# The halves of the row sums added on VectorE in a two-layer decoder trunk: four products per norm in place of eight

## The chip, the cores and the metric

The kernel runs on one core of one Trainium2 chip. The metric is device time in microseconds (us) of one launch; where several runs are given, their median. Engines are named as in the profile: PE (TensorE matmul), PEld (its weight loads), DVE (VectorE), ACT (ScalarE), POOL (GpSimd) and SP (SyncE).

## The reference

The input is one sequence of 512 tokens with 1024 channels, fp32. Cut to what matters here:

```
def rms_norm(x, g):
    xf = x.astype(jnp.float32)
    y = xf * lax.rsqrt(jnp.mean(xf * xf, axis=-1, keepdims=True) + EPS)
    return (y * g.astype(jnp.float32)).astype(x.dtype)

Each layer (DEPTH = 2):
  h = RMSNorm(x)
  p = h @ W_in      (mixer A: chunked spatial gating; mixer B: latent attention with
                     a rotary key; mixer C: gated DeltaNet with a short causal conv;
                     three merge gates)
  y_i = branch_i(p) @ W_branch[i]
  x = x + (sum_i sigmoid(gate_i) * y_i) @ W_out
  x = x + W2 relu(W1 RMSNorm(x))^2
```

Two norms per layer take the mean of the squares of each token's 1024 channels: four norms in all, called norm 0 (input of layer 0), norm 1 (feed-forward of layer 0), norm 2 (input of layer 1) and norm 3 (feed-forward of layer 1). The change concerns how these sums of squares are completed.

## The kernel before, in words

**Layout and products.** Tokens lie on the free axis: a projection gives a PSUM tile of 128 channels x 512 tokens. Each fp32 factor is split in a high part and the rest (`hHi`/`hLo` for the activations, `wHi`/`wLo` for the weights), and each product is three matmuls (L662 to L664). A projection tile takes 8 steps of three, 24 matmuls of 128x512. Tiles of the combined input projection come in a fixed order: tile 0 ("misc": decay, beta and rotary key rows), tiles 1 to 4 (`k`), 5 to 8 (`q`), 9 to 12 (`v`), and so on. From tile 5 on they use two PSUM banks in turn: `project` (L709 on) waits on `bank_read[n % 2]` until the last tile in that bank has been read, so tile 7 starts after the third reading of an odd tile, which are tiles 1, 3 and 5.

**Weights.** They stream from memory in units of 512 KB into `wraw` (two slots). POOL makes of each unit the high part `wHi` (L562, a tensor_scalar) and the rest `wLo` (L567, a tensor_tensor of `wraw` and `wHi`) in a ring of four slots, as fast as units land and slots come free.

**The norm.** PE transposes the stream 128x128 at a time (L681), ACT makes `hHi` (L1344), DVE `hLo` (`stream_low`, L1801), and the projections begin before the norm's factor is known: it is multiplied in when DVE reads a projection tile. ACT squares the rows of the untransposed stream in two halves of 512 channels (L1332), and its accumulator leaves one sum per token and half in `rowsq[P, 2, TT]` (128 partitions, 2 halves, 4 token tiles). `sum_stream` (L684) then waits for all eight squares of the norm and, for each of the four token tiles, multiplies the column `rowsq[:, half, t]`, broadcast to 128x128, by the identity, for both halves into the same PSUM columns: the two halves are added in PSUM, and every partition receives the row of the 128 tokens' sums. From that ACT makes `rstdT` (L1360 a logarithm, L1362 an exponential), and signals `rstd_ready`.

```
for t in range(TT):
    for half in range(2):
        last = mm(S(2)[:, t * P:(t + 1) * P], rowsq[:, half, t:t + 1].broadcast_to([P, P]), ident, start=half == 0, stop=half == 1)
```

**DVE's program at the start.** The order of the work is written out by hand, one program per engine, and each engine executes its program in order, waiting on semaphores. DVE makes `hLo` (L1801 x8), then a triangular table `tri` (L1844), `lowrow` (L1845, L1847), and `rotation_angles(0)` (L1820 to L1837: a cast and seven small operations of 128x64, each waiting for the one before). Then it waits for `rstd_ready` and reads tile 0 (`xrow` L1898, `krT` L1900, L1902). `conv(i)` then takes the tiles k0 to k3, q0 to q3 and v0 in turn: it scales the PSUM tile by `rstdT` (L1909), multiplies it by the last tap (L1913), adds three shifted products (L1916 x3) and counts `bank_read`. Behind `conv(0)` stands L1944, behind `conv(2)` L1947, L1948 and L1950 (the decay rows), behind `conv(5)` a few copies and `rotation_angles(1)`. So tile 7's `bank_read` count of three is reached when `conv(4)` ends.

**Other norms.** In norms 1 and 3 DVE adds the residual (`add_stream`, L1808) half by half and makes four `hLo` tiles after each half; in norm 2 it makes all eight after the last feed-forward group.

**Memory.** The tiles of SBUF are placed in order; `FRONT` and `BACK` are paddings that keep the tiles behind them at fixed places.

Of the kernel before, what the change touches and what calls it, by code (L numbers as in the profile page):

```python
# [10 lines left out]
ALU = mybir.AluOpType  # L11
# [4 lines left out]
P = 128  # L16
# [3 lines left out]
TT = SEQ // P  # L20
# [112 lines left out]
LOW, STACK = 32, 32 + HEADS  # L133


FRONT, BACK = 1664, 348


PRM = {}
# [25 lines left out]
class PerLayer:  # L165
# [3 lines left out]

    y_stored = 16; prm_loaded = 16; x_loaded = 16  # L170

    h_lo = 16; h_high = 16; rows_squared = 16; stat_summed = 2; rl_done = 2; rstd_ready = 2

    act_tile = 12; csq_ready = 8; csq_summed = 2; ksum_copied = 2; ksum_turned = 2

# [37 lines left out]
def hybrid_trunk(nc, stream, params, x, positions, constants, out):  # L213

    with ExitStack() as ctx:
        def sb(name, shape, dt=F32):
            return ctx.enter_context(nc.sbuf_tensor(name, shape, dt))

        def sem(name):
            return ctx.enter_context(nc.semaphore(name))  # L220
# [18 lines left out]
        headstat = sb("headstat", [P, 3, TT * HEADS])  # L239
        negmax, unused = sb("negmax", [P, 2]), sb("unused", [P, 2])  # L240
        psums, pinv = sb("psums", [P, 2, HEADS]), sb("pinv", [P, 2, HEADS])
        rowsq = sb("rowsq", [P, 2, TT])


        sb("back", [P, BACK // 4])
# [59 lines left out]
        def c(name, i=0, n=None, parts=P):  # L305
            a, b = CST[name]
            return cst[0:parts, a + i * (n or 0):(a + (i + 1) * n if n else b)]

        def p(name, i=None, parts=P):
            a, b = PRM[name]  # L310
            return prm[0:parts, a:b] if i is None else prm[0:parts, a + i:a + i + 1]

        ident = c("ident")
# [13 lines left out]
        y_stored, prm_loaded, x_loaded = sem("y_stored"), sem("prm_loaded"), sem("x_loaded")  # L327

        h_lo, h_high, rows_squared = sem("h_lo"), sem("h_high"), sem("rows_squared")
        stat_summed, rl_done, rstd_ready = sem("stat_summed"), sem("rl_done"), sem("rstd_ready")  # L330

        act_tile, csq_ready, csq_summed = sem("act_tile"), sem("csq_ready"), sem("csq_summed")
# [93 lines left out]
        def sums_bank(d):  # L426

            return ps[:, 2 + d % 6]

        def stream_bank(norm, d):  # L430

            return ps[:, (4, 5, 4, 5, 6, 7, 2, 3)[d]] if norm % 2 else sums_bank(d)

        def halves(half):

            return np.s_[half * 512:(half + 1) * 512]
# [214 lines left out]
        def _(pe):  # L651
            pe.wait_ge(ident_in, 16)
            for layer in range(DEPTH):
                mm = nc.tensor.matmul

                def S(n):
                    return ps[:, 2 + n]

                def passes(o, l, lc, r, rc, start, stop):

                    (lh, ll), (rh, rl) = l, r
                    mm(o, lh[lc], rh[rc], start=start, stop=False)  # L662
                    mm(o, lh[lc], rl[rc], start=False, stop=False)  # L663
                    return mm(o, ll[lc], rh[rc], start=False, stop=stop)  # L664
# [18 lines left out]

                def sum_stream(norm):  # L684

                    pe.wait_ge(rows_squared, 8 * norm + 8)
                    pe.wait_ge(h_lo, 8 * norm + 3)
                    for t in range(TT):
                        for half in range(2):
                            last = mm(S(2)[:, t * P:(t + 1) * P], rowsq[:, half, t:t + 1].broadcast_to([P, P]), ident, start=half == 0, stop=half == 1)  # L690
                    last.then_inc(stat_summed, 1)

                def wide_sums(half, kk):
# [293 lines left out]
                if layer == 0:  # L987
                    turn_stream(0, range(0, 4))
                    high_step(0, 0)
                    high_step(0, 1)  # L990
                    turn_stream(0, range(4, 6))
                    high_step(1, 0)
                    high_step(1, 1)
                    high_step(0, 2)
                    turn_stream(0, range(6, KD))
                    high_step(1, 2)
                    for k in range(3, KD):
                        high_step(0, k)
                        high_step(1, k)
                        if k >= 4:  # L1000
                            low_step(0, 2 * k - 8)
                            low_step(0, 2 * k - 7)
                    sum_stream(0)
                    for k in range(KD):
                        low_step(1, k)
                else:
                    project(("misc", 0))
                    sum_stream(2 * layer)
# [35 lines left out]
                for t in range(TT):  # L1044
                    last = nc.tensor.transpose(S(4)[:, t * ROPE:(t + 1) * ROPE], krT[:, t * P:(t + 1) * P], c("ident", parts=ROPE)[:, 0:ROPE])
# [6 lines left out]
                for t in range(TT):  # L1052
                    last = mm(S(3)[32 * t:32 * t + 32, 0:P], c("ones")[:, 0:32], klsq[:, 1, t * P:(t + 1) * P], start=True, stop=True)
# [3 lines left out]
                for t in range(TT + 1):  # L1057
                    last = nc.tensor.transpose(S(5)[:, t * P:(t + 1) * P] if t < TT else S(4)[:, P:2 * P], lsums[:, t * P:(t + 1) * P], ident)
# [12 lines left out]
                for n in range(2):  # L1071
# [3 lines left out]
                    for t in range(TT):  # L1075
# [3 lines left out]
                        for k in range(2):  # L1079
                            last = passes(S(g % 4), (latHi, latLo), np.s_[:, 3 + k, t * P:(t + 1) * P],  # L1080
                                          (wHi, wLo), np.s_[:, slot, k * 512:(k + 1) * 512], k == 0, k == 1)
# [184 lines left out]
                ff1(0, range(0, 4))  # L1266
                turn_stream(2 * layer + 1, range(4, KD))
                sum_stream(2 * layer + 1)
                ff1(1, range(0, 4))
                ff1(0, range(4, KD))  # L1270
# [505 lines left out]
        def _(dve):  # L1776
# [10 lines left out]
            def sums_ready(d, full, done):  # L1787

                if d % 4 < 3:
                    dve.wait_ge(sums_full, full + d // 4 * 3 + d % 4 + 1)  # L1790
                else:
                    dve.wait_ge(unit_done, done + d // 4 * 4 + 4)

            def stream_low(norm, columns=range(KD)):

                gain = "g2" if norm % 2 else "g1"
                if norm % 2 == 0:
                    dve.wait_ge(prm_loaded, 16 * (norm // 2 + 1))
                for d in columns:
                    dve.wait_ge(h_high, 8 * norm + d + 1)  # L1800
                    nc.vector.scalar_tensor_tensor(hLo[:, d], stream_bank(norm, d), p(gain, d), hHi[:, d].bitcast(F32), ALU.mult, ALU.subtract).then_inc(h_lo, 1)  # L1801

            def add_stream(half, full, done):

                for t in range(TT):
                    sums_ready(4 * half + t, full, done)
                    part = y[:, t, halves(half)]
                    nc.vector.tensor_tensor(part, part, sums_bank(4 * half + t), ALU.add).then_inc(x_added, 1)  # L1808

            def zero_rows():  # L1810

                nc.vector.memset(rowsr[0:64].bitcast(F32), 0.0)
                nc.vector.memset(gone[:], 0.0).then_inc(vector_step, 1)
                dve.wait_ge(vector_step, steps.next())

            def rotation_angles(n):
# [22 lines left out]
                assert n == 0 or turns.n == ROPE_STEPS, turns.n  # L1839

            zero_rows()
            stream_low(0)
            dve.wait_ge(tables_in, 48)
            nc.vector.tensor_scalar(tri[:], c("incl"), -1.0, None, ALU.is_ge).then_inc(tri_done, 1)  # L1844
            nc.vector.reduce_sum(lowrow[:], c("ident")[0:2 * HEADS, HEADS:2 * HEADS], AX.X).then_inc(vector_step, 1)  # L1845
# [4 lines left out]
            for layer in range(DEPTH):  # L1850
# [439 lines left out]
                dve.wait_ge(x_loaded, layer * per.x_loaded + 16)  # L2290
                for half in range(2):
                    add_stream(half, layer * per.sums_full, layer * per.unit_done + UNIT_NO[("out", 0)])
                    stream_low(2 * layer + 1, range(4 * half, 4 * half + 4))

                def rectify(n):
# [88 lines left out]
                if layer < DEPTH - 1:  # L2384
                    zero_rows()
# [6 lines left out]
                add_corner(g, "p3", Y, 0, 1, ALU.subtract, (g, "p6"))  # L2392
                if layer < DEPTH - 1:
                    stream_low(2 * layer + 2)


# [122 lines left out]
```

## Time and profile before

| | |
|---|---|
| runs | 1763.55, 1764.39, 1763.82 us; median 1763.82 |
| profiled execution, its own time | 1764.11 us |
| its span | 1762.3 us |
| granted TensorE clock | 1.00 |
| PE busy | 1744.1 us, 99% of the span |
| POOL / DVE / ACT busy | 1066.3 / 958.8 / 689.9 us |

The profile is of one execution. Its page gives each engine's busy time, the span in 40 slices, and the chain of work that ended last. The answers of the trace are lists of single instructions (the timeline), of waits, and of groups. In the timeline an instruction that is held up once it has started shows as longer than its like; an engine that waits on a semaphore shows as idle, in brackets with what released it.

### The profile page before, as it was taken

To read this page: it belongs to the slowest core of one execution; us is meant where nothing else is said; L and a number is where in the kernel's file an instruction comes from. 1 tells how busy PE (TensorE), PEld (TensorE's weight loads), DVE (VectorE), ACT (ScalarE), POOL (GpSimd) and SP (SyncE) were. 2 spreads that over 40 slices of the span, in tenths; PEclk is the share of its full clock that TensorE was granted. 3 is DMA by queue.
4 is the path that set the end of the run, shared out by engine and by line. 5 is a ranking of instruction groups with operands and counts; after the bars stand their busy time and mean duration, and the time that the engine had idled before them with its cause. 6 is when DMAs were issued, how large, how long until landed. Compare 5 with 4: busy or idle time off the path is not lost.

```text
span 1762.3 us, 26300 instructions
## 1 busy us (share of the span) xinstructions
PE 1744.1 (99%) x10006; PEld 1426.3 (81%) x10006; DVE 958.8 (54%) x1565; ACT 689.9 (39%) x1241; POOL 1066.3 (61%) x572
## 2 busy tenths in 40 slices
PE   8999999999999999999999999999999999999999
PEld 7778888778888888888787788887788888888887
DVE  6786636653542455444576866266443435444445
ACT  6433316650104444444355243075411054444442
POOL 6444367235665777777774434662456657777776
PEclk9999999999999999999999999999999999999999
DMA  6222133123235666666542222331332356666655
GB/s 201 85 69 77 49 96 108 37 96 96 84 97 169 157 172 161 161 174 157 130 156 78 71 70 61 96 96 37 108 96 85 97 158 163 159 173 158 169 154 144
DMA packets 58897, 207.18 MB, mean 118 GB/s; under 512 B 6369, under 2 KB 8705, under 8 KB 58785
## 3 DMA queue, kind: packets, MB, share of 16 engines
q1 hardware_dynamic: 47520, 164.94, 29.9%
q0 software_dynamic: 9216, 33.56, 10.2%
q10 hardware_dynamic: 2048, 7.10, 1.1%
q8 instruction: 80, 1.31, 0.3%
q14 instruction: 33, 0.26, 0.0%
HBM read 184.61 MB, written 4.19 MB: 107 GB/s over the span
## 4 chain that ended last, share of the span: by engine, by line
PE 95%; ACT 2%; DVE 2%; issue 1%; DMA 0%; SPq 0%; DVEq 0%; ACTq 0%
PE ps L662 22%; PE ps L664 22%; PE ps L663 22%; PE ps L1259 6%; PE ps L1261 6%; PE ps L1260 6%; PE ps L1131 2%; PE ps L1140 1%; PE ps L1153 1%; PE ps L681 1%; PE ps L904 1%; PE ps L891 0%; DMA xin<-x 0%; PE ps L941 0%; PE ps L1203 0%
## 5 line engine op out<-in xcount | busy, mean ns | idle before, releaser
L662 PE MATMUL ps<-hHi,wHi 128*128 128x512 f32 x1360 | 553.2, 407 | 1.3 <-DVE convd L1916 1.3
L664 PE MATMUL ps<-hHi,wLo 128*128 128x512 f32 x1360 | 530.4, 390 | 0.0
L663 PE MATMUL ps<-hLo,wHi 128*128 128x512 f32 x1360 | 529.8, 390 | 0.0
L562 POOL TENSOR_SCALAR wHi<-wraw 128x1024 fp32r<-128x1024 f32 x168 | 181.4, 1080 | 497.3 <-PE ps L664 480.2
L567 POOL TENSOR_TENSOR wLo<-wraw,wHi 128x1024 fp32r<-128x1024 f32 x168 | 415.2, 2472 | 13.9
L593 POOL TENSOR_TENSOR wLo<-w,wHi 128x1024 fp32r<-128x1024 f32 x96 | 239.2, 2514 | 138.6 <-ACT wHi L1690 138.0
L662 PEld LDWEIGHTS ps<-hHi,wHi 128*128 128x128 f32 x1360 | 255.4, 188 | 61.5 <-issue 6.9
L663 PEld LDWEIGHTS ps<-hLo,wHi 128*128 128x128 f32 x1360 | 255.7, 188 | 54.7 <-issue 3.8
L664 PEld LDWEIGHTS ps<-hHi,wLo 128*128 128x128 f32 x1360 | 255.3, 188 | 54.2
L1259 PE MATMUL ps<-wHi,fHi 128*128 128x512 f32 x448 | 174.8, 390 | 1.8 <-issue 1.8
L1260 PE MATMUL ps<-wLo,fHi 128*128 128x512 f32 x448 | 174.3, 389 | 0.0
L1261 PE MATMUL ps<-wHi,fLo 128*128 128x512 f32 x448 | 174.3, 389 | 0.0
L593 POOL TENSOR_TENSOR wLo<-wraw,wHi 128x1024 fp32r<-128x1024 f32 x56 | 144.3, 2576 | 14.2 <-ACT wHi L1690 14.2
L2302 DVE SCALAR_TENSOR_TENSOR relu<-ps,rstdT 128x512 f32<-128x512 f32 x64 | 44.2, 691 | 187.0 <-PE ps L664 187.0
L1709 ACT ACTIVATE ps<-relu 128x512 f32<-128x512 f32 x64 | 38.5, 602 | 269.9 <-DVE relu L2302 269.9
L1396 ACT ACTIVATE sg<-ps 128x512 f32<-128x512 f32 x48 | 28.8, 599 | 255.7 <-DVE ps L1859 255.7
L2337 DVE TENSOR_TENSOR y<-y,ps 128x1024 f32<-128x1024 f32 x98 | 116.7, 1212 | 6.7 <-PE ps L1261 6.5
L1690 ACT CAST wHi<-w 128x1024 fp32r<-128x1024 f32 x96 | 99.5, 1043 | 22.4 <-DMA w<-w 18.9
L1259 PEld LDWEIGHTS ps<-wHi,fHi 128*128 128x128 f32 x448 | 84.1, 188 | 20.7 <-issue 2.8
L1859 DVE TENSOR_TENSOR ps<-ps,rstdT 128x512 f32<-128x512 f32 x56 | 38.9, 698 | 111.2 <-PE ps L664 111.0
L1261 PEld LDWEIGHTS ps<-wHi,fLo 128*128 128x128 f32 x448 | 84.1, 188 | 17.5
L1260 PEld LDWEIGHTS ps<-wLo,fHi 128*128 128x128 f32 x448 | 84.1, 188 | 17.3
(334 smaller groups left out, 2675.0 us busy)
## 6 DMA issues: line engine op xcount, KB each, us to landing
wraw<-stream SPq DMA_DIRECT2D x224, 512.0 KB, 3.6
w<-stream SPq DMA_DIRECT2D x64, 512.0 KB, 4.4
w<-w POOLq DMA_DIRECT2D x32, 512.0 KB, 6.9
b<-stream SPq DMA_DIRECT2D x16, 512.0 KB, 3.5
b<-stream POOLq DMA_DIRECT2D x16, 512.0 KB, 6.4
w<-stream POOLq DMA_DIRECT2D x16, 512.0 KB, 8.1
xin<-x SPq DMA_DIRECT2D x4, 512.0 KB, 6.8
y<-x ACTq DMA_DIRECT2D x1, 2048.0 KB, 9.9
```

Of the source, the lines that this page charges most:

```text
L562: nc.gpsimd.tensor_scalar(wHi[:, slot], wraw[:, slot % RAW], 1.0, 0.0, ALU.mult, ALU.add).then_inc(unit_high, 1)
L567: nc.gpsimd.tensor_tensor(wLo[:, slot], wraw[:, slot % RAW], wHi[:, slot].bitcast(F32), ALU.subtract).then_inc(unit_split, 1)
L593: nc.gpsimd.tensor_tensor(wLo[:, at % RING], source, wHi[:, at % RING].bitcast(F32), ALU.subtract).then_inc(unit_split, 1)
L662: mm(o, lh[lc], rh[rc], start=start, stop=False)
L663: mm(o, lh[lc], rl[rc], start=False, stop=False)
L664: return mm(o, ll[lc], rh[rc], start=False, stop=stop)
L1259: mm(ps[:, bank + i], fHi[b][tokens], wHi[cols], start=opens and k == 0, stop=False, skip_group_check=True)
L1260: mm(ps[:, bank + i], fHi[b][tokens], wLo[cols], start=False, stop=False, skip_group_check=True)
L1261: last = mm(ps[:, bank + i], fLo[b][tokens], wHi[cols], start=False, stop=k == 1, skip_group_check=True)
L1690: nc.scalar.copy(wHi[:, at % RING], source).then_inc(high_copied, 1)
L2302: stt(relu[:, n % 2], tile_home(n), 0.0, rstdT[:], ALU.max, ALU.mult).then_inc(vector_tile, 1)
L2337: tt_(part, part, ps[:, bank:bank + 2], op).then_inc(corner_added, 1)
```

## The change

A new tile `rowsum[P, TT]` (16 bytes per partition) holds the sum of both halves. DVE adds them (`sum_rows`), once per norm, and counts a new semaphore, `rows_summed`; PE's `sum_stream` waits for that in place of `rows_squared` and makes one product for each token tile. `BACK` is 16 bytes smaller, so the tiles behind it keep their addresses. For norm 0, `sum_rows` stands between the `hLo` tiles and `tri`; for norms 1 and 3 between the second half's residual additions and its `hLo` tiles; for norm 2 behind the `hLo` tiles.

```diff
-FRONT, BACK = 1664, 348
+FRONT, BACK = 1664, 332
...
-        rowsq = sb("rowsq", [P, 2, TT])
+        rowsq, rowsum = sb("rowsq", [P, 2, TT]), sb("rowsum", [P, TT])
...
                 def sum_stream(norm):
 
-                    pe.wait_ge(rows_squared, 8 * norm + 8)
+                    pe.wait_ge(rows_summed, norm + 1)
                     pe.wait_ge(h_lo, 8 * norm + 3)
                     for t in range(TT):
-                        for half in range(2):
-                            last = mm(S(2)[:, t * P:(t + 1) * P], rowsq[:, half, t:t + 1].broadcast_to([P, P]), ident, start=half == 0, stop=half == 1)
+                        last = mm(S(2)[:, t * P:(t + 1) * P], rowsum[:, t:t + 1].broadcast_to([P, P]), ident, start=True, stop=True)
                     last.then_inc(stat_summed, 1)
...
+            def sum_rows(norm):
+
+                dve.wait_ge(rows_squared, 8 * norm + 8)
+                if norm:
+                    dve.wait_ge(stat_summed, norm)
+                nc.vector.tensor_tensor(rowsum[:], rowsq[:, 0], rowsq[:, 1], ALU.add).then_inc(rows_summed, 1)
+
...
             zero_rows()
             stream_low(0)
+            sum_rows(0)
             dve.wait_ge(tables_in, 48)
             nc.vector.tensor_scalar(tri[:], c("incl"), -1.0, None, ALU.is_ge).then_inc(tri_done, 1)
...
                     add_stream(half, layer * per.sums_full, layer * per.unit_done + UNIT_NO[("out", 0)])
+                    if half:
+                        sum_rows(2 * layer + 1)
                     stream_low(2 * layer + 1, range(4 * half, 4 * half + 4))
...
                 if layer < DEPTH - 1:
                     stream_low(2 * layer + 2)
+                    sum_rows(2 * layer + 2)
```

The order of the instructions shows what that moves. First PE's, at norm 0, between the last steps of the first tiles; - is before, + the change, and `cst` is the table that holds the identity:

```order
 L731 MATMUL ps<-hLo,wHi 128x512
 L736 MATMUL ps<-hHi,wLo 128x512 x2
-L690 MATMUL ps<-cst,rowsq 128x128 x8
+L690 MATMUL ps<-cst,rowsum 128x128 x4
 L736 MATMUL ps<-hHi,wLo 128x512 x8
```

Four products are gone there, and in the same way at each of the other three norms.

Second DVE's at norm 0, before the change, with the semaphores that each instruction waits for:

```order
L1801 SCALAR_TENSOR_TENSOR hLo<-ps,prm,hHi 128x512 [waits h_high] x7
L1844 TENSOR_SCALAR tri<-cst 128x128 [waits tables_in]
L1845 TENSOR_REDUCE lowrow<-cst 16x1
L1847 TENSOR_SCALAR lowrow<-lowrow 16x1 [waits vector_step]
L1820 CAST posf<-posi 128x4 [waits tables_in,vector_step]
L1824 TENSOR_TENSOR gy<-posf,cst 128x64 [waits rope_step]
L1827 TENSOR_SCALAR gy<-gy 128x64 [waits rope_step]
L1829 TENSOR_SCALAR gy<-gy 128x64 [waits rope_step]
L1832 SCALAR_TENSOR_TENSOR gy<-gy 128x64 [waits rope_step] x3
L1837 TENSOR_SCALAR trig<-gy 128x64 [waits rope_step]
L1898 SCALAR_TENSOR_TENSOR xrow<-ps,sgn,rstdT 40x512 [waits rstd_ready,unit_done,rope_step]
```

And the same stretch with the change:

```order
L1801 SCALAR_TENSOR_TENSOR hLo<-ps,prm,hHi 128x512 [waits h_high] x7
L1815 TENSOR_TENSOR rowsum<-rowsq 128x4 [waits rows_squared]
L1852 TENSOR_SCALAR tri<-cst 128x128 [waits tables_in]
L1853 TENSOR_REDUCE lowrow<-cst 16x1
L1855 TENSOR_SCALAR lowrow<-lowrow 16x1 [waits vector_step]
L1827 CAST posf<-posi 128x4 [waits tables_in,vector_step]
L1831 TENSOR_TENSOR gy<-posf,cst 128x64 [waits rope_step]
L1834 TENSOR_SCALAR gy<-gy 128x64 [waits rope_step]
L1836 TENSOR_SCALAR gy<-gy 128x64 [waits rope_step]
L1839 SCALAR_TENSOR_TENSOR gy<-gy 128x64 [waits rope_step] x3
L1844 TENSOR_SCALAR trig<-gy 128x64 [waits rope_step]
L1906 SCALAR_TENSOR_TENSOR xrow<-ps,sgn,rstdT 40x512 [waits rstd_ready,unit_done,rope_step]
```

The eleven small instructions now stand behind the addition, and so behind its wait for ACT's eighth square.

Third DVE's at norm 1 with the change; norm 3 reads the same:

```order
L1808 TENSOR_TENSOR y<-y,ps 128x512 [waits sums_full] x3
L1808 TENSOR_TENSOR y<-y,ps 128x512 [waits unit_done]
L1815 TENSOR_TENSOR rowsum<-rowsq 128x4 [waits stat_summed,rows_squared]
L1801 SCALAR_TENSOR_TENSOR hLo<-ps,prm,hHi 128x512 [waits h_high] x4
L2312 SCALAR_TENSOR_TENSOR relu<-ps,rstdT 128x512 [waits rstd_ready,unit_done]
```

The addition is the one new row; four `hLo` tiles stand behind it. At norm 2 it follows the last `hLo` tile. The programs of ACT, POOL and SP are the same as before.

## Rows read from the trace of the kernel before

**Rows 1.** The page: busy times, granted clock in 40 slices, the chain by engine

```profile
PE 1744.1 (99%) x10006; PEld 1426.3 (81%) x10006; DVE 958.8 (54%) x1565; ACT 689.9 (39%) x1241; POOL 1066.3 (61%) x572
...
PEclk9999999999999999999999999999999999999999
...
PE 95%; ACT 2%; DVE 2%; issue 1%; DMA 0%; SPq 0%; DVEq 0%; ACTq 0%
```

**Rows 2.** Waits of PE: engine, line, cause: us in total, times, longest

```profile
PE ps L662 <- DVE convd L1916: 1.3, 2, 0.6
```

**Rows 3.** Instructions that read rowsq: count, duration ns min/median/max, first and last start

```profile
L690 PE MATMUL ps<-cst,rowsq x64: 271/275/275, 20.9 to 1433.5; 128*128 128x128 f32 x64
```

**Rows 4.** Chain that ended last, norm 0: start us, us, what

```profile
21.07 1.78 PE ps L690 x16
```

**Rows 5.** Timeline of PE at norm 0: start us, us, instruction

```profile
20.91 1.95 PE L690 MATMUL ps<-cst,rowsq 128*128 128x128 f32 x16
22.61 2.09 PE L736 MATMUL ps<-hHi,wLo 128*128 128x512 f32 x8
```

**Rows 6.** Timeline of ACT and DVE at norm 0: [idle before <-releaser] in brackets

```profile
18.66 0.20 ACT L1332 ACTIVATION_READ_ACCUMULATOR squares<-xin 128x1 f32 x1
...
16.51 0.22 DVE L1844 TENSOR_SCALAR tri<-cst 128x128 f32<-128x128 f32 x1
...
25.66 0.74 DVE L1898 SCALAR_TENSOR_TENSOR xrow<-ps,sgn,rstdT 40x512 f32<-40x512 f32 x1 [6.77 <-ACT rstdT L1362]
```

**Rows 7.** Timeline of POOL, 18 to 34 us

```profile
18.95 1.05 POOL L562 TENSOR_SCALAR wHi<-wraw 128x1024 fp32r<-128x1024 f32 x1 [3.58 <-DMA wraw<-stream]
20.09 2.36 POOL L567 TENSOR_TENSOR wLo<-wraw,wHi 128x1024 fp32r<-128x1024 f32 x1
...
23.54 2.40 POOL L567 TENSOR_TENSOR wLo<-wraw,wHi 128x1024 fp32r<-128x1024 f32 x1
26.24 1.06 POOL L562 TENSOR_SCALAR wHi<-wraw 128x1024 fp32r<-128x1024 f32 x1 [0.30 <-DMA wraw<-stream]
27.38 2.52 POOL L567 TENSOR_TENSOR wLo<-wraw,wHi 128x1024 fp32r<-128x1024 f32 x1
29.86 1.06 POOL L562 TENSOR_SCALAR wHi<-wraw 128x1024 fp32r<-128x1024 f32 x1
31.01 2.40 POOL L567 TENSOR_TENSOR wLo<-wraw,wHi 128x1024 fp32r<-128x1024 f32 x1
```

**Rows 8.** L1902 in both layers, and POOL beside the second (timeline)

```profile
L1902 DVE TENSOR_SCALAR xrow<-xrow,prm x2: 474/1570/2666, 27.2 to 898.5; 8x512 f32<-8x512 f32 x2
...
898.52 2.40 POOL L567 TENSOR_TENSOR wLo<-wraw,wHi 128x1024 fp32r<-128x1024 f32 x1
```

**Rows 9.** Timeline of DVE, 31 to 53 us

```profile
31.42 2.54 DVE L1944 SCALAR_TENSOR_TENSOR arow<-xrow 40x512 f32<-40x512 f32 x1
...
41.43 1.48 DVE L1948 SCALAR_TENSOR_TENSOR xrow<-xrow,arow 40x512 f32<-40x512 f32 x1
42.94 2.50 DVE L1950 TENSOR_SCALAR xrow<-xrow,slope 40x512 f32<-40x512 f32 x1
...
50.62 2.32 DVE L1916 SCALAR_TENSOR_TENSOR convd<-ps,prm,convd 128x511 f32<-128x511 f32 x3
```

**Rows 10.** Timeline of PE where tile 7 starts

```profile
53.20 0.50 PE L662 MATMUL ps<-hHi,wHi 128*128 128x512 f32 x1
```

**Rows 11.** Timeline of POOL and PE at norm 1

```profile
553.61 2.38 POOL L567 TENSOR_TENSOR wLo<-wraw,wHi 128x1024 fp32r<-128x1024 f32 x1
...
556.56 1.95 PE L690 MATMUL ps<-cst,rowsq 128*128 128x128 f32 x16
```

**Rows 12.** Timeline of POOL and PE at norm 2

```profile
890.89 1.05 POOL L562 TENSOR_SCALAR wHi<-wraw 128x1024 fp32r<-128x1024 f32 x1 [0.55 <-DMA wraw<-stream]
...
892.32 1.95 PE L690 MATMUL ps<-cst,rowsq 128*128 128x128 f32 x16
```

**Rows 13.** Timeline of PE at its first products

```profile
5.49 3.34 PE L681 MATMUL ps<-cst,xin 128*128 128x128 f32 x16 [5.49 <-DMA xin<-x]
```

More of the change, by code:

```diff
@@ L170 @@
     y_stored = 16; prm_loaded = 16; x_loaded = 16
-    h_lo = 16; h_high = 16; rows_squared = 16; stat_summed = 2; rl_done = 2; rstd_ready = 2
+    h_lo = 16; h_high = 16; rows_squared = 16; rows_summed = 2; stat_summed = 2; rl_done = 2; rstd_ready = 2
     act_tile = 12; csq_ready = 8; csq_summed = 2; ksum_copied = 2; ksum_turned = 2
@@ L329, in hybrid_trunk @@
         h_lo, h_high, rows_squared = sem("h_lo"), sem("h_high"), sem("rows_squared")
+        rows_summed = sem("rows_summed")
         stat_summed, rl_done, rstd_ready = sem("stat_summed"), sem("rl_done"), sem("rstd_ready")
```

## The prediction

> **What bounds the kernel now.** I read the page first. PE is busy for 99% of the span at a granted clock of nine tenths or more in all 40 slices, and the chain that ended last runs over PE for 95% [rows 1]. So time is won by fewer PE instructions, and lost where PE is made to wait. The list of PE's waits says how near that is: only the wait on `conv` (L1916) bears on this change, twice and 1.3 us in all, 0.6 us at the longest [rows 2]. DVE has gaps over the whole program (54% busy), but the question is the stretch around norm 0. There I read the timelines of ACT, DVE, POOL and PE side by side [rows 5 to 10].
>
> What bounds the end there is a chain: squares (ACT), sums (PE), `rstdT` (ACT), `xrow` (DVE), then nine `conv`s on DVE, whose fifth releases the bank that PE needs for tile 7. The last piece of `conv(4)` starts at 50.62 and its group of three takes 2.32, so it ends at 52.94; PE starts tile 7 at 53.20 [rows 9, 10]. **The slack is 0.26 us.** From `xrow` on DVE is almost never idle up to there, so what delays `xrow` reaches PE, less what is won back on the way.
>
> A second thing is to be seen there. Some DVE instructions last until a running POOL instruction ends. L1902 (8x512, SBUF to SBUF) takes 0.474 in layer 0 and 2.666 in layer 1, where it starts together with an L567 of 2.40 [rows 8]. L1944 takes 2.54 from 31.42, and the L567 beside it ends at 33.41 [rows 7, 9]. L1948 and L1950, one after the other, take 1.48 and 2.50 [rows 9]: each waits for one POOL instruction. So with both engines at work they take turns, one DVE instruction per POOL instruction. Instructions that read PSUM (L1909, L1913, L1916) show none of it. The Trainium skill, page "SBUF — State Buffer", section "Who interferes with whom", says that VectorE and GpSimd share a pair of SBUF ports as an exclusive lock held for a whole instruction, and that a VectorE operation with two SBUF inputs takes part; the 2.666 against 0.474 agrees.
>
> **The change part by part.**
>
> *Products removed.* There are 64 records of L690, 16 per norm for 8 products, so two records to a product [rows 3]. On the chain 16 cost 1.78 us, 0.111 each [rows 4]; by the timeline the next line starts 1.70 after the first, 0.106 each [rows 5]. Eight fewer records save 0.85 to 0.89 per norm. I take 0.89, and 3.56 for four norms, if each reaches the end.
>
> *Additions at norms 1, 2 and 3.* No row shows a 128x4 addition. The bounds are nothing (hidden) and, for one norm, the 2.40 of an L567 that it falls behind. At norm 1 an L567 runs from 553.61 to 555.99 [rows 11]. The addition ends behind it at about 556.1, and PE comes to the sum at 556.56, or not before: hidden, by 0.4. Norm 3 has the same pattern. The `hLo` tiles behind the addition wait for ACT anyway. At norm 2 the L562 ends at 891.94, and PE comes at 892.32 [rows 12]: hidden again, by 0.3 if the addition is let in between L562 and the next POOL instruction, which the turns above say. PE comes earlier nowhere by more than the norms before have saved, and POOL's work, which follows PE's freeing of slots, moves along. So these three give −0.89 each, **−2.67**. If norm 2's addition lands behind the next L567, of 2.4, the cost is some 1.6 us instead; that goes to a rival.
>
> *The addition at norm 0.* ACT's last square ends at 18.86, and POOL's L562 starts at 18.95 [rows 6, 7]. The addition fits before it, or waits until 20.00. PE comes to the sum at 20.91 [rows 5], so PE is not held up in either case, and `rstdT` comes 0.89 earlier.
>
> *The eleven small instructions moved behind it.* This is the costly part. Before, they start at 16.51 and end by 18.9 [rows 6], while POOL is idle: its L562 at 18.95 had stood 3.58 us idle [rows 7]. They cost nothing, as DVE then waits 6.77 us for `rstdT` [rows 6]. Now they stand behind the addition, and POOL works back to back from 18.95. Their bounds: 2.4 us as before if nothing holds them up, so they end at 21.4 and still cost nothing; or one POOL instruction each. By the turns: `tri` comes behind L562 (20.0), the two `lowrow` pieces of 16 channels by one element beside it, the cast behind L567 (22.45), the first product behind L562 (23.45), the first scaling behind L567 (25.94). In POOL's gap of 0.30 before 26.24 [rows 7] two more slip in. The remaining three come behind 27.30, 29.90 and 30.92. So DVE is free at about **31.0**. I take this end, since the rows on L1948 and L1950 are the nearest, though they are wider (512 elements against 64).
>
> `xrow` then starts at 31.0 in place of 25.66: 5.3 late. From there: `xrow` and `krT` 1.4, then L1902 behind the L567 that ends at 33.41 (before it had met none, 0.47): 33.5 to 33.7, and `conv(0)` is 6.0 late. L1944 was held up before by 1.8 us (2.54 less the 0.74 that the equally large L1898 takes [rows 6, 9]), and now, at 37.4, meets at most the end of an L562 of 1.06: 4.9 late. L1948 and L1950 were held up for 2.8 us in all, by 0.74 and 0.47 alone, and now, shifted against POOL, for some 2.3: 4.4 late. `conv(4)` ends at 57.3 in place of 52.94, and PE starts tile 7 at 57.4 in place of 53.20: **+4.2**. The 0.89 that PE wins at norm 0 is swallowed by this wait, so it is not in the sum.
>
> *Later in layer 0.* `rotation_angles(1)` behind `conv(5)` may now touch a POOL instruction; bounds 0 and 0.9, I take **+0.4**.
>
> *The new padding* leaves the addresses as they are: nothing.
>
> **Sum:** +4.2 + 0.4 − 2.67 = +1.9 us. The profiled execution took 1764.11 us (span 1762.3 and 1.8 around it), 0.29 above the median of the runs; the difference is added to the median 1763.82: **1765.7 us**. A measurement of this kernel can tell 0.2% (3.5 us) from no change, so the lines lie at 1760.3 and 1767.3, and my forecast is in between: no change that can be told, though 1.9 slower.
>
> **The rivals.**
>
> *A. The small instructions are not held up* (or only the addition is): the change does what it says, −3.56 us, **1760.3**. For it: they are short, and no row shows an instruction of 64 elements beside POOL in this stretch. Against: L1902, of 8 channels, was held up for 2.2 us. It is decided by whether DVE is free before 24.8, when `rstdT` now comes. Chance 0.13, of which 0.09 below 1760.3.
>
> *B. Some slip through.* If two or three pass between POOL's instructions, DVE is free at 26 to 27.5 and PE stands still for 0.5 to 1.5: **1761.8** to 1763. Chance 0.10.
>
> *C. A longer lag.* If nothing slips into the gap before 26.24, the last comes behind the L567 that ends at 33.41; `conv(0)` then ends after 40, and PE's tile 5, which takes the bank that it releases, waits as well; or norm 2's addition falls behind L567 (+1.6). Total +3.5 to +4.3: **1767.4 to 1768.1**. For it: two POOL instructions of 2.4 us are only 1.1 apart. Chance 0.12, all on the slower side.
>
> *D. The lag of the forecast, and TensorE's clock falls in it.* This ends slower. PE would stand still for some 4 us ahead of tile 7. Before, it stands so long only at the very start, 5.49 us [rows 13]. That start shows the price: the first 16 records of 128x128 take 3.34 us against 1.95 for 16 of the same shape later [rows 5], so 1.4 us; up to 2.8 if it stays low twice as long. Total +3.3 to +4.7: **1767.1 to 1768.5**. For it: the stop is long. Against: between the stops PE has short products to do (the sums of `csq`), and the granted clock never fell in the 40 slices [rows 1]. It decides from the point where the clock is below 1.0 in the stretch after the stop. The Trainium skill, page "TensorE: Matmul & The Clock Gate", section "What's actually happening", says that the throttled state is the default and that activity releases it, which speaks for D; the slow first products agree. Chance 0.15, slower.
>
> **How the numbers follow.** Forecast 0.50, B 0.10, C 0.12, D 0.15, A 0.13. Slower by over 0.2%: C and D, 0.27. Faster: 0.09. Same: 0.50 + 0.10 + the 0.04 left of A, 0.64. The range starts at 1761.6, just under B, and leaves out A (0.13). At the other end it takes in D's and C's bounds, with 0.5 for the unknown rotation: 1769.0. The forecast's own range is 1764.5 to 1767.0.
>
> **What would show it.** In the profile after: 32 records of L690, four times 0.89 long. DVE's small instructions stretch from 18.9 to about 31, several of them 1 to 2.5 us long and ending with a POOL instruction; `xrow` starts near 31 and waits for nothing; a wait of PE's L662 on L1924 (`conv`) of 4 to 5 us ahead of tile 7, partly before the `csq` sums. If `xrow` starts at 24.8 behind `rstdT`, I am wrong and A is right. If PE's stop is there but the time is over 1767, the clock and norm 2's sum are the places to look: a start later than 893 less the shift of the first half would be the second. From 60 us on everything should run as before, 4 to 5 us late, until norms 1 to 3 give 0.89 each back.

## The result, and the profile after

The changed kernel takes 1779.62 us (median of six runs, 1777.8 to 1785.19) against 1764.01 us for the kernel before (median of six, 1763.55 to 1765.66). The ratio is 1.0092, 95% interval 1.0082 to 1.0102: **slower by 0.9%**, where 1765.7 was forecast. The profiled execution took 1785.19 us (span 1783.3), the slowest of the six and 21.1 us above the profiled execution of before. The runs lie 7 us apart, those of before 2. The granted clock on record is 0.998 for the profiled run, 0.999 for one other (1780.38) and 1.000 for the remaining four, so the profile shows the second loss below at its largest, not as the median has it.

The page of the changed kernel, busy times and granted clock, answers to [rows 1]:

```profile
PE 1760.4 (99%) x9974; PEld 1424.6 (80%) x9974; DVE 971.2 (54%) x1569; ACT 690.0 (39%) x1241; POOL 1067.8 (60%) x572
...
PEclk9999999999999999999999999999999999999999
```

PE has 32 instructions fewer, and is busy for 16.3 us more. Waiting is the smaller part of the loss. The list of PE's waits (us in total, times, longest), which answers to [rows 2]:

```profile
PE ps L682 <- DMA xin<-x: 5.0, 1, 5.0
PE ps L746 <- ACT csq L1419: 4.5, 1, 4.5
PE ps L663 <- DVE convd L1924: 1.8, 3, 0.7
...
PE ps L1259 <- DVE y L2347: 1.1, 1, 1.1
```

The stop of 4.5 us ahead of the `csq` sums is new, and so is the last row shown. The products are gone as the diff says (tile `rowsum`, answers to [rows 3]):

```profile
L690 PE MATMUL ps<-cst,rowsum x32: 271/275/275, 20.8 to 1450.4; 128*128 128x128 f32 x32
L1815 DVE TENSOR_TENSOR rowsum<-rowsq x4: 625/1440/2249, 18.8 to 1446.9; 128x4 f32<-128x4 f32 x4
```

**First loss: norm 0's chain.** The timelines of DVE and of POOL, which answer to [rows 6, 7]:

```profile
18.80 0.62 DVE L1815 TENSOR_TENSOR rowsum<-rowsq 128x4 f32<-128x4 f32 x1 [2.31 <-ACT squares L1332]
19.34 0.21 DVE L1852 TENSOR_SCALAR tri<-cst 128x128 f32<-128x128 f32 x1
19.48 0.14 DVE L1853 TENSOR_REDUCE lowrow<-cst 16x1 f32<-16x8 f32 x1
19.65 0.14 DVE L1855 TENSOR_SCALAR lowrow<-lowrow 16x1 f32<-16x1 f32 x1
19.83 2.07 DVE L1827 CAST posf<-posi 128x4 f32<-128x4 int32 x1
21.94 1.03 DVE L1831 TENSOR_TENSOR gy<-posf,cst 128x64 f32<-128x64 f32 x1
23.00 2.44 DVE L1834 TENSOR_SCALAR gy<-gy 128x64 f32<-128x64 f32 x1
25.47 0.20 DVE L1836 TENSOR_SCALAR gy<-gy 128x64 f32<-128x64 f32 x1
25.70 4.57 DVE L1839 SCALAR_TENSOR_TENSOR gy<-gy 128x64 f32<-128x64 f32 x3
30.30 2.43 DVE L1844 TENSOR_SCALAR trig<-gy 128x64 f32<-128x64 f32 x1
32.76 0.74 DVE L1906 SCALAR_TENSOR_TENSOR xrow<-ps,sgn,rstdT 40x512 f32<-40x512 f32 x1
```
```profile
18.37 1.04 POOL L563 TENSOR_SCALAR wHi<-wraw 128x1024 fp32r<-128x1024 f32 x1 [3.37 <-DMA wraw<-stream]
19.50 2.38 POOL L568 TENSOR_TENSOR wLo<-wraw,wHi 128x1024 fp32r<-128x1024 f32 x1
...
22.98 2.41 POOL L568 TENSOR_TENSOR wLo<-wraw,wHi 128x1024 fp32r<-128x1024 f32 x1
...
30.28 2.40 POOL L568 TENSOR_TENSOR wLo<-wraw,wHi 128x1024 fp32r<-128x1024 f32 x1
```

Most of the small instructions wait, one after another, for a POOL instruction: the cast ends at 21.90 with the L568 that ends at 21.88, L1834 at 25.44 with the one that ends at 25.39, the last at 32.73 with the one that ends at 32.68. `xrow` starts at 32.76, 7.1 us later than before, and waits for nothing.

**Second loss: TensorE's clock.** The end of `conv(4)` in DVE's timeline, PE's timeline ahead of tile 7, then the stretches of 4 us (busy time of each engine, granted clock, DMA share, GB/s):

```profile
56.40 2.32 DVE L1924 SCALAR_TENSOR_TENSOR convd<-ps,prm,convd 128x511 f32<-128x511 f32 x3
```
```profile
56.35 1.94 PE L746 MATMUL ps<-csq,cst 128*32 128x512 f32 x8 [4.50 <-ACT csq L1419]
58.22 0.65 PE L760 MATMUL ps<-cst,xrow 40*128 40x40 f32 x4
58.80 0.79 PE L663 MATMUL ps<-hHi,wHi 128*128 128x512 f32 x1
59.39 0.63 PE L664 MATMUL ps<-hLo,wHi 128*128 128x512 f32 x1
...
61.87 0.40 PE L664 MATMUL ps<-hLo,wHi 128*128 128x512 f32 x1
```
```profile
50.00:54.00 4.00, 1.85 (x9) 1.19 (x7) 3.86 (x6) 0.72 (x2) 1.95 (x3) 1.00 0.39 133
54.00:58.00 4.00, 1.65 (x8) 0.20 (x8) 3.82 (x7) 1.26 (x2) 1.61 (x1) 0.62 0.31 60
58.00:62.00 4.00, 4.00 (x16) 3.08 (x13) 3.86 (x6) 1.73 (x3) 0.00 (x0) 0.53 0.18 73
```

The stop itself belongs to the first loss: PE waits for ACT's squares of the `k` tiles, which wait for `conv(3)`. During it the granted clock falls from 1.00 to about half, the lower of its two levels (1.2 GHz), and stays there through the first products behind it: 0.63 us for a matmul in place of 0.40. The page's slices of 45 us don't show it. Tile 7 starts at 58.80 in place of 53.20 [rows 10], 5.6 us late. At full clock it could not have come sooner, as `conv(4)` ends only at 58.72. By 64 us the same instructions come 7.0 us late, so the slow clock costs **1.4 us**, all of it behind the start of tile 7.

**Third loss, and the largest: the pace of the matmuls.** Twelve matmuls of a feed-forward corner, first and last, of the kernel before and then of the changed one (timeline of PE, ten rows left out in each):

```profile
1501.69 0.39 PE L1259 MATMUL ps<-wHi,fHi 128*128 128x512 f32 x1
...
1504.19 0.39 PE L1261 MATMUL ps<-wHi,fLo 128*128 128x512 f32 x1
```
```profile
1519.26 0.39 PE L1259 MATMUL ps<-wHi,fHi 128*128 128x512 f32 x1
...
1521.82 0.40 PE L1261 MATMUL ps<-wHi,fLo 128*128 128x512 f32 x1
```

Eleven steps take 2.50 us before, 227 ns each, and 2.56 after, 233 each. No engine waits. The groups of the page show where it holds (count | busy, mean ns), before and after:

```profile
L662 PE MATMUL ps<-hHi,wHi 128*128 128x512 f32 x1360 | 553.2, 407 | 1.3 <-DVE convd L1916 1.3
L1259 PE MATMUL ps<-wHi,fHi 128*128 128x512 f32 x448 | 174.8, 390 | 1.8 <-issue 1.8
L664 PE MATMUL ps<-bHi,wLo 128*128 128x512 f32 x192 | 74.7, 389 | 0.0
```
```profile
L663 PE MATMUL ps<-hHi,wHi 128*128 128x512 f32 x1360 | 554.5, 408 | 1.8 <-DVE convd L1924 1.8
L1259 PE MATMUL ps<-wHi,fHi 128*128 128x512 f32 x448 | 177.2, 396 | 2.5 <-issue 1.4 <-DVE y L2347 1.1
L665 PE MATMUL ps<-bHi,wLo 128*128 128x512 f32 x192 | 75.9, 395 | 0.0
```

Products of `hHi` with `wHi` keep their pace. Those of `wHi` with `fHi`, `bHi`, `mHi` or `latHi` are slower, in all twelve such groups; their busy times add up to 14.9 us more. The tiles `f`, `b`, `m` and `lat` all lie behind the padding `back`. The new tile has 16 bytes and the padding is 16 smaller, but tiles are placed on multiples of 32 bytes: before, 348 bytes took 352; now 16 take 32 and 332 take 352. Everything behind moved by **32 bytes**.

For the profiled execution the account, by the starts of the same PE instructions in both timelines, is: 0.1 us earlier when norm 0 begins, norm 0's stretch +7.0 (−0.9 for the products, then the stop and the slow clock), three norms −2.7, a late DVE instruction of the feed-forward near 791 us +1.4 (experiment 4), and the pace +15.4, which is what experiment 2 has from norm 0 to the end. That is +21.0, and the spans differ by 21.0. The groups' busy times show 14.9 of the 15.4.

### The profile page after: what moved, and what is told of

Read it like the earlier page. It is cut to its first block, busy times and chain, and to the rows that moved or that the text cites. A ratio compares the mean times of both kernels' runs of the same rounds, so it can differ in the third digit from the quotient of the medians.

```text
span 1783.3 us, 26243 instructions
## 1 busy us (share of the span) xinstructions
PE 1760.4 (99%) x9974; PEld 1424.6 (80%) x9974; DVE 971.2 (54%) x1569; ACT 690.0 (39%) x1241; POOL 1067.8 (60%) x572
## 4 chain that ended last, share of the span: by engine, by line
PE 93%; DVE 3%; ACT 2%; issue 1%; DMA 0%; POOL 0%; SPq 0%; DVEq 0%; ACTq 0%; POOLq 0%
PE ps L663 22%; PE ps L665 21%; PE ps L664 21%; PE ps L1259 6%; PE ps L1261 6%; PE ps L1260 6%; PE ps L1131 2%; PE ps L1140 1%; PE ps L1153 1%; DVE convd L1924 1%; PE ps L682 1%; PE ps L904 1%; PE ps L891 0%; PE ps L941 0%; PE ps L1203 0%
## 5 line engine op out<-in xcount | busy, mean ns | idle before, releaser
L568 POOL TENSOR_TENSOR wLo<-wraw,wHi 128x1024 fp32r<-128x1024 f32 x168 | 415.8, 2475 | 13.8
L1259 PE MATMUL ps<-wHi,fHi 128*128 128x512 f32 x448 | 177.2, 396 | 2.5 <-issue 1.4
L1261 PE MATMUL ps<-wHi,fLo 128*128 128x512 f32 x448 | 177.2, 396 | 0.0
L1259 PEld LDWEIGHTS ps<-wHi,fHi 128*128 128x128 f32 x448 | 84.1, 188 | 23.7 <-issue 3.7
L1261 PEld LDWEIGHTS ps<-wHi,fLo 128*128 128x128 f32 x448 | 84.1, 188 | 20.2
```

Of the source, the lines that this page charges most:

```text
L568: nc.gpsimd.tensor_tensor(wLo[:, slot], wraw[:, slot % RAW], wHi[:, slot].bitcast(F32), ALU.subtract).then_inc(unit_split, 1)
L1259: mm(ps[:, bank + i], fHi[b][tokens], wHi[cols], start=opens and k == 0, stop=False, skip_group_check=True)
L1261: last = mm(ps[:, bank + i], fLo[b][tokens], wHi[cols], start=False, stop=k == 1, skip_group_check=True)
```

## The experiments

Each was run beside the kernel before on one chip, whose median was 1763.8 to 1764.1 us in the three series.

**1. The homes put back.** The changed kernel, with

```diff
-FRONT, BACK = 1664, 332
+FRONT, BACK = 1664, 316
```

> The changed kernel with a padding of 316 bytes in place of 332. Theory H (homes): tiles are placed on multiples of 32 bytes, so the new tile of 16 bytes took 32, and everything behind the padding moved by 32 bytes (from a multiple of 64 to an odd multiple of 32); PE reads such tiles at some 233 ns a matmul in place of 227, worth 14 to 15 us over the program. With 316 the homes are back: every matmul at 226 to 227 ns, median 1764.5 to 1768.5 us (the late DVE chain of norm 0, +7.0 in the trace, less 2.7 for three norms, is left, +4.3). Theory P (PE's pace follows from its own program, which is shorter by 16 products or waits on another semaphore): the slow pace stays, 1777 to 1781 us.

Measured: 1767.16 us median of ten (1760.67 to 1769.82), ratio 1.0015 (1.0005 to 1.0025). L1259 to L1261 are back at 227 ns:

```profile
L1259 PE MATMUL ps<-wHi,fHi 128*128 128x512 f32 x448 | 174.8, 390 | 3.1 <-issue 1.7 <-DVE y L2347 1.4
```

Theory H holds. This is the change as it was meant: 3.4 us slower by medians, not faster. In its profile (1765.60, granted clock 0.999) `xrow` starts at 29.90, since here two of the small instructions found gaps, and PE stops twice, for 1.8 and 1.0 us:

```profile
52.20 1.07 PE L746 MATMUL ps<-csq,cst 128*32 128x512 f32 x8 [1.80 <-ACT csq L1419]
...
54.63 0.80 PE L663 MATMUL ps<-hHi,wHi 128*128 128x512 f32 x1 [0.99 <-DVE convd L1924]
```

How many find gaps differs from profile to profile. The times fall in line with the granted clock: seven of the ten runs have 0.998 and take 1765.97 to 1769.82, the profiled one has 0.999, and the two at 1.000 take 1760.67 and 1764.59. So in most runs the clock fell for longer than in the profiled one.

**2. The homes moved, nothing else.** The kernel before, with

```diff
-FRONT, BACK = 1664, 348
+FRONT, BACK = 1664, 380
```

> The kernel before with a padding of 380 bytes in place of 348: nothing else differs, and all homes behind it move by 32 bytes. Theory H: half of the matmuls (those of L1259 to L1261 and those that read the branch and merge tiles) at 231 to 235 ns, 14 to 15 us slower than before, 1777.5 to 1779.5 us. Theory P: 1764 us, as before.

Measured: 1780.21 us (four runs, 1779.31 to 1780.86), ratio 1.009 (1.0073 to 1.0106). Eight products, no addition, no stop, and **16.4 us** slower by medians with 32 bytes of place as the only edit. In the profiled run (1780.79) the start took its part: PE's first products stayed at the lower clock for longer (L731 0.63 us at 9.64, before 0.39 at 9.87), and it comes to norm 0's sum 1.3 us late, before any product that reads a home. The pace is worth the other **15.4 us**:

```profile
L1259 PE MATMUL ps<-wHi,fHi 128*128 128x512 f32 x448 | 177.2, 395 | 1.5 <-issue 1.5
```

The two effects don't add up by medians: 16.4 and 3.4 make 1783.8, and the change has 1779.6. The granted clocks go with that: below 1.000 in eight of experiment 1's ten runs, in two of the change's six. So most of the change's runs show no fall of the clock, and most of experiment 1's do. Why it came less often in the change, with the same order of work at norm 0, wasn't tried.

**3. The wait alone.** The kernel before, with

```diff
             stream_low(0)
+            dve.wait_ge(rows_squared, 8)
             dve.wait_ge(tables_in, 48)
```

> The kernel before with one wait more on DVE: for ACT's eighth square, ahead of the triangular table, where the addition stands in the change. No addition, eight products, homes as before. Theory L (the lag of the eleven small instructions among POOL's): xrow starts at 31 to 33 in place of 25.7, PE stops for 3.5 to 5 us ahead of its tile 7 and starts again at half its clock, in all +5.5 to +7.5 us, 1769.5 to 1771.5. Rival (the addition itself, or PE's new wait on DVE, brings the loss): within 1 us of before.

Measured: 1768.91 us (seven runs, 1765.38 to 1772.1), ratio 1.0022 (1.001 to 1.0034); the profiled run, 1771.03, shows the whole course: `xrow` at 32.67, a stop of 4.5 us, the clock at half (0.50 from 58 to 62 us). The seven runs are two groups: four with a granted clock of 0.998 take 1768.91 to 1772.1, three at 1.000 take 1765.38 to 1766.27.

```profile
30.21 2.42 DVE L1837 TENSOR_SCALAR trig<-gy 128x64 f32<-128x64 f32 x1
32.67 0.74 DVE L1899 SCALAR_TENSOR_TENSOR xrow<-ps,sgn,rstdT 40x512 f32<-40x512 f32 x1
```
```profile
56.21 1.94 PE L746 MATMUL ps<-csq,cst 128*32 128x512 f32 x8 [4.52 <-ACT csq L1419]
```

So neither the addition nor PE's wait on DVE is needed for the loss: what counts is when the small instructions start. Theory L holds in its course; the median lies 0.6 us under the range that was expected, as three of the runs show no fall of the clock.

**4. The addition behind the small instructions.** Experiment 1, with

```diff
             stream_low(0)
-            sum_rows(0)
...
             rotation_angles(0)
+            sum_rows(0)
```

> The changed kernel with a padding of 316 bytes and with norm 0's addition behind the eleven small instructions, not ahead of them. Theories H and L together: the small instructions run before POOL starts, the addition waits at most for POOL's first instruction (to 20.0), PE is not held up, and only the gain is left: four norms at 0.89, 1764.0 - 3.6 = 1760.4 us (1760.0 to 1761.2). If the addition falls behind POOL's second instruction, PE waits for 1.5 us at norm 0: 1762.

Measured: 1762.58 us (ten runs, 1761.29 to 1769.39), ratio 0.9998 (0.9988 to 1.0007). In the profiled run (1761.65) the stop and the clock's fall are gone, and the addition takes 0.85 us, hidden. Two of the ten runs, 1765.11 and 1769.39, still have a granted clock of 0.999:

```profile
18.23 0.85 DVE L1815 TENSOR_TENSOR rowsum<-rowsq 128x4 f32<-128x4 f32 x1
24.01 0.74 DVE L1906 SCALAR_TENSOR_TENSOR xrow<-ps,sgn,rstdT 40x512 f32<-40x512 f32 x1 [4.93 <-ACT rstdT L1362]
```

But 2.2 us of the expected gain are missing by the median. In the trace tile 7 gives back 0.4 us, and 1.8 go in one place, a DVE instruction of the feed-forward that is held up through three of POOL's (DVE, then POOL):

```profile
1479.94 7.13 DVE L2337 TENSOR_TENSOR fLo<-mixed,fHi 128x768 fp32r<-128x768 f32 x1
```
```profile
1478.53 5.37 POOL L594 TENSOR_TENSOR wLo<-w,wHi 128x1024 fp32r<-128x1024 f32 x2
1483.30 2.95 POOL L594 TENSOR_TENSOR wLo<-wraw,wHi 128x1024 fp32r<-128x1024 f32 x1
```

**5. The homes moved by 64 bytes** (the kernel before, `BACK` 412).

> The kernel before with a padding of 412 bytes in place of 348: the homes behind it move by 64 bytes, and stay on multiples of 64. Theory H64 (what costs is a start on an odd multiple of 32 bytes): matmuls at 226 to 227 ns and 1763 to 1765.5 us, as before. Rival (any other place of the homes costs, the old one being tuned): 231 to 235 ns and some 1780 us, as with 32 bytes.

Measured: 1778.31 us (two runs, 1778.24 and 1778.39), ratio 1.0081 (1.0063 to 1.01). Theory H64 falls: a multiple of 64 is not enough. One group kept its pace here, `bLo` with `wHi` (mean 389 ns as before), and `bHi` with `wLo` lost half of what the others lost (392).

**6. The front moved by 32 bytes, the homes kept** (the kernel before).

```diff
-FRONT, BACK = 1664, 348
+FRONT, BACK = 1696, 316
```

> The kernel before with the front padding 32 bytes larger and the back padding 32 smaller: the homes behind the back padding stay, while the activations hHi and hLo, the weights wHi and wLo and the small tables move to odd multiples of 32 bytes. Theory H64: now nearly every matmul of the program reads such a tile, some 5500 of 128x512; at 6.3 ns more each, +35 us, 1795 to 1802 us. If only one of the two operands counted (the streamed or the loaded one), a part of the lines would keep 227 ns and the time would lie between 1770 and 1790. Rival (only the homes behind the back padding matter): 1764.

Measured: 1779.19 us (two runs, 1779.08 and 1779.31), ratio 1.0086 (1.0068 to 1.0105), not 1795. The products of two front tiles keep their pace though both moved; those of a front tile and a home are slow again:

```profile
L662 PE MATMUL ps<-hHi,wHi 128*128 128x512 f32 x1360 | 553.5, 407 | 1.2 <-DVE convd L1916 1.2
L1259 PE MATMUL ps<-wHi,fHi 128*128 128x512 f32 x448 | 177.1, 395 | 1.3 <-issue 1.3
```

Both the theory and its rival fall. The third case on record, that only one of the two operands counts, gives a time in this range too, but it would have slowed lines with two front tiles, as both had moved. What counts, as far as these runs go, is the **distance between the two tiles** that a matmul reads, not the place of either.

**7 and 8. Which norms.** Experiment 4 with four products at norms 0 and 2 alone, and at 1 and 3 alone; in 8 norm 0 has no addition.

> The kernel of e4 (homes back, norm 0's addition behind the small instructions), but with four products at norms 0 and 2 alone; norms 1 and 3 keep eight products and no addition. Theory S (sum): 1764.0 less twice 0.89, 1762.2 us. Theory W (the shorter sums of norms 1 and 3 shift PE against the weight stream of the feed-forward, and there DVE's fLo instruction of 128x768 loses three turns to POOL, as at 1479.94 us in e4's trace, 2.1 us of PE's time): no instruction of that line takes more than 2.1 us here, the runs are as close together as those of before (within 2.7 us of each other, e4: 8.1), and the median is not above e4's 1762.6.

> The same with four products at norms 1 and 3 alone; norms 0 and 2 keep eight products and no addition, and the small instructions start at 16.5 us as before. Theory S: 1762.2 us. Theory W: at least one fLo instruction of 128x768 takes about 7 us, runs differ by more than 4 us, and the median is 1763 to 1765: the gain of 1.8 is given back there.

Measured: 7 takes 1762.44 us (eleven runs, 1761.52 to 1766.69), ratio 0.9996 (0.9987 to 1.0005). 8 takes 1761.96 (eleven, 1761.27 to 1763.53), ratio 0.999 (0.9981 to 0.9999). Both medians agree with the sum. The spread forecast for 7 (2.7 us) doesn't: its runs lie 5.2 us apart. Theory W falls: in 8 no `fLo` instruction takes more than 2.06 us, and it is the tighter of the two. The scattered runs belong to 7, which touches norm 0: its three above 1765 us are the three with a granted clock of 0.999, all others of both experiments have 1.000.

**9 and 10. The distance in larger steps** (the kernel before, `BACK` 220 and 92).

> The kernel before with a padding of 220 bytes in place of 348: the homes behind it move by 128 bytes. The runs so far say that it is the distance between the two tiles that a matmul reads, not the place of either: moving only the front by 32 bytes slowed the same matmuls as moving only the homes, and left those that read two front tiles alone. Before, that distance is a multiple of 512 bytes. Theory D128 (a distance of a multiple of 128 is enough): 226 to 227 ns, 1764 us. Theory D256 or more: 231 to 235 ns for L1259 to L1261, 1778 to 1781 us.

> The same with a padding of 92 bytes: the homes move by 256 bytes. If a multiple of 256 is enough, 1764 us, and with a slow run of 128 bytes the step is 256; if this one is slow as well, the step is 512 or more, 1778 to 1781 us.

Measured, one run each: 1779.16 us with 128 bytes, 1763.95 with 256, with these groups:

```profile
L1259 PE MATMUL ps<-wHi,fHi 128*128 128x512 f32 x448 | 177.5, 396 | 1.5 <-issue 1.5
```
```profile
L1259 PE MATMUL ps<-wHi,fHi 128*128 128x512 f32 x448 | 174.7, 390 | 1.8 <-issue 1.7
```

So of 0, 32, 64, 128 and 256 bytes only 0 and 256 have every group at full pace.

**11 and 12. Three norms against four.** 11 leaves norm 0 as it was and has four products at the other three:

```diff
+                    if norm:
+                        pe.wait_ge(rows_summed, norm)
+                    else:
+                        pe.wait_ge(rows_squared, 8 * norm + 8)
```

12 is experiment 4 once more.

> Homes back, four products at norms 1, 2 and 3, norm 0 as before (eight products, no addition). Sum: 1764.0 less three times 0.89, 1761.4 us, with runs as close together as those of the kernel before, since the tight chain of norm 0 keeps its timing. If instead the products are worth less than the chain says, 1762.5 or more.

> The kernel of e4 once more, beside e11 on one chip: four norms. By the sum 1760.4 us; by e4's runs 1762.6, with some above 1765, because norm 0's chain on DVE meets POOL at another phase and the slack ahead of PE's tile 7 is 0.26 us. If e11 is the faster or the tighter of the two, norm 0 is best left alone.

Measured: 11 takes **1760.7 us** (eleven runs, 1760.3 to 1761.13), ratio 0.9982 (0.9973 to 0.9991); 12 takes 1761.94 (eleven, 1759.88 to 1767.66), ratio 0.999 (0.9981 to 0.9999). 11 is the faster by its median, and its runs lie 0.8 us apart, those of 12 7.8. It beats the kernel before by 3.1 us by medians, a little more than three times 0.89. One run of 12 is the fastest of all, so the fourth norm's 0.89 is there. What takes it back is seen in the two profiles of that kernel: 0.3 to 0.4 us ahead of tile 7, and 1.8 (experiment 4) or 3.4 us (12, where PE is held up twice) at the long `fLo` instruction. In the other runs of 12 it isn't separated; two have a granted clock of 0.999. The two intervals overlap, so that 11 is steadier is surer than that it is faster. The long `fLo` instruction was in all four profiles with four products at every norm (the change, 1, 4 and 12; 6.9 to 7.4 us) and in no other. What sets it off is open.

## Why the prediction was wrong, by its own steps

- **"The new padding leaves the addresses as they are: nothing."** This is the step that failed. It took the diff's arithmetic for the layout. The same belief stands in the section on the change, and it is wrong there too. The homes moved by 32 bytes, and that alone costs 16.4 us by medians, 15.4 of them PE's pace (experiment 2); putting them back gives 1767.2 (experiment 1), inside the range of 1761.6 to 1769.0. No case of mine had a price on PE's own pace.
- **Products removed: 0.85 to 0.89 per norm.** Right: 32 records, and experiments 7, 8 and 11 give 1.6, 2.1 and 3.1 us for two, two and three norms.
- **Additions at norms 1 to 3 hidden.** Right in its result. They take up to 2.25 us behind POOL, and experiment 11 has the whole gain.
- **The addition at norm 0 holds PE up in neither case.** Right: 0.62 us from 18.80, and the sum starts at 20.8.
- **The small instructions wait for one POOL instruction each, DVE free at 31.0.** The mechanism was right, and so were the held-up steps up to 25.4. The size varies: 32.7 in the change's trace and in experiment 3 (one slipped into the gap before 25.61, not two), 29.9 in experiment 1. The forecast value is in the middle.
- **PE stops, tile 7 at 57.4.** It started at 58.80. The surplus is DVE's lag, mis-sized: `conv(4)` ends at 58.72, where 57.3 was worked out, as `xrow` started 1.8 us later than forecast. The test at the end asked for a wait on `conv` (L1924) of 4 to 5 us, partly before the `csq` sums; the whole stop stood ahead of them, on ACT's `csq`, a step that the chain of the prediction leaves out.
- **Rival D, the clock falls in the stop.** It did, to about half, and cost 1.4 us: tile 7 is 5.6 us late, the instructions of 64 us are 7.0 late; what the `csq` sums lost by it was hidden behind `conv(4)`. It was priced at 1.4 to 2.8, so the lower bound came true. I gave it 0.15; in the two traces with a stop of 4.5 us the clock fell, and in that of experiment 1 too, with 1.8 us (0.57 from 54 to 58 us). The granted clocks of the runs have it below 1.000 in two of six runs of the change, eight of ten of experiment 1 and four of seven of experiment 3. The page "TensorE: Matmul & The Clock Gate" of the Trainium skill, section "What's actually happening", has the throttled state as the default that activity lifts; these stretches agree. "The granted clock never fell in the 40 slices" was a poor argument, as before had no stop there.
- **Rival C, a longer lag.** It came true in the profiled run of the change: the last small instruction ends with the POOL instruction that ends at 32.68 (33.41 before), and PE's tile 5 waits 0.7 us, the third wait on L1924 in the list. Its condition didn't quite, as one instruction did slip into a gap. I gave it 0.12. Rival B, DVE free at 26 to 27.5, is in none of the profiles.
- **Rival A, not held up.** Wrong for the change, and right once the addition stands behind (experiment 4): the order in DVE's program, not the length of the instructions, decides.
- **The reading of L1902.** Its 2.666 against 0.474 us shows a hold-up beside POOL, but it is an operation on one tile, so it says nothing of operations with two SBUF inputs, for which the prediction brought it up. L1948 and the addition (0.62 to 2.25 us) have two.
- **The rotation behind `conv(5)`, +0.4:** nothing of it reached PE. The same PE instructions are 7.0 us late at 64 us and 6.9 at 110, and in experiment 3 7.4 at both.

The working of the change without the moved homes was +1.9 us; experiment 1 gives +2.7 by the ratio and +3.4 by medians. That this lies in the range is in part luck: the runs with the clock's fall take 1765.6 to 1769.8, the two without it 1760.7 and 1764.6, and the forecast lies between the two groups. Had I asked what the allocator does with 16 bytes, I would have known that the homes move; that the move costs 2.8% on some 2400 matmuls no row of before could show.

## What to carry to other kernels

Check the addresses, not the diff, when a tile is added, and look at PE's start-to-start time first when a profile grows evenly: a few nanoseconds per matmul over thousands are more than any wait. An addition that waits for another engine belongs behind the work that needs nothing, above all where that work runs in a gap of an engine that holds it up later. A saving on the bound engine is worth its full price only where the chain behind it has slack; here leaving the one tight norm alone was steadier, and faster by its median, than changing all four. And look at how a kernel's runs are spread before reading its one profile: the granted clock of each run tells whether the profiled one is like the median.

## What the runs showed of the hardware

- A 128x512 matmul starts every 227 ns when its two tiles lie in the same position against each other as before, or 256 bytes off, and every 232 to 236 ns (medians of the groups) when they are 32, 64 or 128 bytes off, whichever of them moved (experiments 1, 2, 5, 6, 9, 10). Before, by the sizes in the kernel, `wHi` and the homes are a multiple of 256 bytes apart. There is a finer part that wasn't tried: with 64 bytes one group kept its pace (`bLo` with `wHi`, 226 ns) and one came to 229 (`bHi` with `wLo`). The products of `latHi` and `latLo` of 128x384 kept their 173 to 174 ns with the homes moved by 32, but took 175 to 177 with the front moved by 32 or the homes by 128. Why the distance counts no run shows.
- Around a stop of 1.8 us on PE and another of 1.0 close behind (experiment 1), the granted clock was 0.57 from 54 to 58 us, and a 128x512 matmul took 0.63 us; with one stop of 4.5 us it was 0.53 from 58 to 62 us (the change).
- DVE and POOL mostly take turns, but a DVE instruction of 128x768 with two SBUF inputs lost three turns in a row and took 7.13 us in place of 1.64 (experiment 4).
